# A fused two-block transformer kernel: the start distance of the activation tiles in SBUF, 1024 bytes to 1056 and 2048 to 2080

## What is computed

```python
def first_block(x, ...):
    for l in range(DEPTH):                       # DEPTH = 2
        h = rms_norm(x, norm_mix[l])
        proj = h @ w_in[l]                       # 1024 -> 5120
        ...                                      # two attentions
        mixed = gates[..., :D_MODEL] * y_a + gates[..., D_MODEL:] * y_b
        x = x + mixed @ w_out[l]                 # 1024 -> 1024
        h = rms_norm(x, norm_ffn[l])
        x = x + conv_ffn(h, w_up[l], conv_w[l], conv_b[l], w_down[l])   # 1024 -> 5632, 2816 -> 1024
    return rms_norm(x, norm_final)

def hybrid_layer(x, ...):
    proj = rmsnorm(x, norm_mix_w) @ w_in
    ...                                          # delta rule, recurrence
    x = x + concatenate([gdn_out, lru_out]) @ w_out
    u = jax.nn.relu(rmsnorm(x, norm_mlp_w) @ w_ff1)                     # 1024 -> 4096
    return x + (u * u) @ w_ff2                                          # 4096 -> 1024
```

## Time and profile before

| | us |
|---|---|
| median of three runs | 1054.52 |
| lowest, highest | 1054.43, 1056.76 |
| the profiled execution | 1053.14 |
| its span, first to last instruction | 1051.3 |
| TensorE busy in it | 1038.7 |
| VectorE, ScalarE, GpSimd busy | 719.9, 574.1, 287.2 |

### The profile page before, as it was taken

The page is one execution under the profiler, slowest core; times in us unless marked ns, Lnnn a source line. Parts: engine busy times, 40 slices in busy tenths (PEclk is TensorE's granted clock), DMA queues, the critical chain, the costliest instruction groups (busy, mean ns, idle before and its releaser), DMA issues.

```text
span 1051.3 us, 20017 instructions
## 1 busy us (share of the span) xinstructions
PE 1038.7 (99%) x8398; PEld 984.1 (94%) x8398; DVE 719.9 (68%) x1217; ACT 574.1 (55%) x791; POOL 287.2 (27%) x179
## 2 busy tenths in 40 slices
PE   8999999999999999999999999999999999999997
PEld 7999998999999899999999989998999999899996
DVE  5762248787688775322788967877888789666663
ACT  6454466655355644445765544556658875343443
POOL 0376675100000137666740000013400035001120
PEclk9999999999999999999999999999999999999999
DMA  9644454465763664344455566456432157664841
GB/s 308 202 158 154 157 166 161 161 215 159 228 200 126 208 224 164 124 158 140 156 186 189 173 225 215 133 152 220 122 114 89 61 181 230 191 210 131 261 160 40
DMA packets 169705, 180.11 MB, mean 171 GB/s; under 512 B 4240, under 2 KB 166416, under 8 KB 169488
## 3 DMA queue, kind: packets, MB, share of 16 engines
q1 hardware_dynamic: 169616, 178.84, 52.8%
HBM read 177.78 MB, written 1.05 MB: 170 GB/s over the span
## 4 chain that ended last, share of the span: by engine, by line
PE 84%; DVE 8%; ACT 4%; POOL 2%; issue 1%; DMA 1%; SPq 0%; POOLq 0%; ACTq 0%; DVEq 0%
PE psum L679 83%; DVE sb_w_lo L1861 3%; POOL sb_w_lo L2615 1%; ACT sb_scratch L1329 1%; ACT sb_w_hi L1329 1%; DVE psum L1845 1%; DVE sb_xg_lo L1845 1%; POOL sb_scratch L2655 1%; DVE sb_scratch L1845 1%; DMA sb_raw<-in_w_in 1%; PE psum L906 1%; DVE sb_xt L1879 0%; DVE sb_xt L1877 0%; ACT L1329 0%; DVE sb_hid_both L1936 0%
## 5 line engine op out<-in xcount | busy, mean ns | idle before, releaser
L1329 ACT ACTIVATE sb_w_hi<-sb_raw 128x2048 fp32r<-128x2048 f32 (+3 forms) x185 | 318.7, 1727 | 162.0 <-PE psum L679 98.6
L679 PE MATMUL psum<-sb_xg_hi,sb_w_hi 128*128 128x256 f32 x1656 | 401.8, 283 | 0.4 <-DVE psum L1845 0.3
L679 PE MATMUL psum<-sb_xg_lo,sb_w_hi 128*128 128x256 f32 x1656 | 396.7, 279 | 0.0
L1861 DVE TENSOR_TENSOR sb_w_lo<-sb_raw,sb_w_hi 128x2048 fp32r<-128x2048 f32 (+3 forms) x150 | 305.9, 2042 | 104.4 <-ACT sb_w_hi L1329 103.3
L679 PEld LDWEIGHTS psum<-sb_xg_hi,sb_w_hi 128*128 128x128 f32 x1656 | 310.2, 187 | 3.7 <-issue 0.9
L679 PEld LDWEIGHTS psum<-sb_xg_lo,sb_w_hi 128*128 128x128 f32 x1656 | 310.7, 188 | 0.3
L679 PE MATMUL psum<-sb_xg_hi,sb_w_lo 128*128 128x256 f32 x1656 | 228.4, 280 | 1.0 <-DVE sb_w_lo L1861 0.9
L679 PE MATMUL psum<-sb_hid_both,sb_w_hi 128*128 128x512 f32 (+1 forms) x912 | 210.4, 364 | 0.7 <-DVE sb_hid_both L1936 0.4
L679 PEld LDWEIGHTS psum<-sb_xg_hi,sb_w_lo 128*128 128x128 f32 x1656 | 207.9, 187 | 2.0 <-DVE sb_w_lo L1861 1.4
L2615 POOL TENSOR_TENSOR sb_w_lo<-sb_raw,sb_w_hi 128x2048 fp32r<-128x2048 f32 (+1 forms) x34 | 156.0, 4594 | 107.3 <-ACT sb_w_hi L1329 97.9
L679 PEld LDWEIGHTS psum<-sb_hid_both,sb_w_hi 128*128 128x128 f32 x912 | 148.7, 188 | 22.2 <-DVE sb_hid_both L1936 1.2
(11 more groups left out here) (172 smaller groups left out, 988.4 us busy)
## 6 DMA issues: line engine op xcount, KB each, us to landing
sb_raw<-in_w_in SPq DMA_DIRECT2D x51, 1024.0 KB, 5.2
sb_raw<-in_w_up SPq DMA_DIRECT2D x44, 1024.0 KB, 5.1
sb_raw<-in_w_ff SPq DMA_DIRECT2D x21, 1024.0 KB, 5.6
sb_raw<-in_w_down SPq DMA_DIRECT2D x16, 768.0 KB, 4.9
sb_raw<-in_w_down SPq DMA_DIRECT2D x16, 640.0 KB, 4.4
sb_raw<-in_w_out SPq DMA_DIRECT2D x8, 1024.0 KB, 5.2
sb_raw<-in_w_ff SPq DMA_DIRECT2D x8, 768.0 KB, 4.6
sb_raw<-in_w_ff SPq DMA_DIRECT2D x8, 640.0 KB, 4.5
```

What stands on the lines that cost most here:

```text
L679: return nc.tensor.matmul(ps, lhsT, rhs, start=start, stop=stop, skip_group_check=True)
L1329: return nc.scalar.activation(out_, in_, func, **kw)
L1861: v.tensor_tensor(part(w_lo, s), part(raw, s), part(w_hi, s).bitcast(F32), ALU.subtract)\
```

## The change

`XPITCH = 264` is the distance, in columns, from one tile of `xg_hi` (and of `xg_lo`) to the next: 1056 bytes instead of 1024. Tile i of either is now `xg_of(buf, i)`, the 256 columns from 264·i on; the eight columns between tiles are not used. A pair of `hid_both` begins every 520 columns, 2080 bytes instead of 2048; inside a pair the high and the low part still touch. The writers (ScalarE's copy, VectorE's subtraction) and the readers (`xg_parts`, `hid_pair`) go to the new places. `xg_full`, `xt`, the weights and all else keep their form.

The three buffers grow by 256, 256 and 384 bytes in a partition. `xg_lo` now begins at byte 33152 and `hid_both` at 41600, and everything behind them (`w_hi` and `w_lo` among it) lies 896 bytes higher; `w_lo` ends at 226528. Every engine has the same instructions in the same order with the same waits; only addresses differ.

```diff
--- before.py
+++ after.py
@@ -91,6 +91,7 @@
 RAWS = 1
 IDLE_TURNS = 12
 SLAB = 2048
+XPITCH = 264
 RING = 3
 BANK_SC, BANK_T, BANK_O = 3, 5, 7
 
@@ -405,9 +406,9 @@
             return ctx.enter_context(nc.sbuf_tensor("sb_" + name, [P, cols], dt))[:, :]
 
         xt = sb("xt", KD * T)
-        xg_hi = sb("xg_hi", KD * T, F32R)
-        xg_lo = sb("xg_lo", KD * T, F32R)
-        hid_both = sb("hid_both", 2 * HID * T, F32R)
+        xg_hi = sb("xg_hi", KD * XPITCH, F32R)
+        xg_lo = sb("xg_lo", KD * XPITCH, F32R)
+        hid_both = sb("hid_both", HID * (T + XPITCH), F32R)
         cst = sb("consts", CONSTS.shape[1])
         par = sb("params", PARAM_COLS["cols"])
         sq = sb("sq", 4 * T)
@@ -512,9 +513,13 @@
 
             return plan.banks[plan.at[t][0]][-1] + 1
 
+        def xg_of(buf, i):
+
+            return buf[:, i * XPITCH:i * XPITCH + T]
+
         def hid_pair(i):
 
-            return tl(hid_both, i, 2 * T)
+            return hid_both[:, i * (T + XPITCH):i * (T + XPITCH) + 2 * T]
 
         def hid_hi(i):
             return hid_pair(i)[:, 0:T]
@@ -523,7 +528,7 @@
             return hid_pair(i)[:, T:2 * T]
 
         def xg_parts(i):
-            return tl(xg_hi, i), tl(xg_lo, i)
+            return xg_of(xg_hi, i), xg_of(xg_lo, i)
 
         def hid_parts(first=0):
             return lambda i: (hid_hi(first + i), hid_lo(first + i))
@@ -1369,13 +1374,13 @@
 
                 act.wait_ge(S["x_tile"], q.next("x_tile"))
                 if square_gain:
-                    f(tl(xg_hi, m), tl(xt, m), ACT.Copy, scale=gain(m)).then_inc(S["xg_hi"], 1)
+                    f(xg_of(xg_hi, m), tl(xt, m), ACT.Copy, scale=gain(m)).then_inc(S["xg_hi"], 1)
                 for n in range(2 if square_gain else 1):
                     square_room(m, 2 if square_gain else 1, n)
                     kw = {} if n == 0 else {"scale": square_gain(m)}
                     f(tl(sq, 2 * n + m % 2), tl(xt, m), ACT.Square, **kw).then_inc(S["square"], 1)
                 if not square_gain:
-                    f(tl(xg_hi, m), tl(xt, m), ACT.Copy, scale=gain(m)).then_inc(S["xg_hi"], 1)
+                    f(xg_of(xg_hi, m), tl(xt, m), ACT.Copy, scale=gain(m)).then_inc(S["xg_hi"], 1)
 
             def guess():
 
@@ -1401,7 +1406,7 @@
                 f(tl(xg_full, m), tl(xt, m), ACT.Copy, scale=col("norm_mix0", m)).then_inc(S["xg_full"], q.one("xg_full"))
             for m in range(KD):
                 act.wait_ge(S["xg_full"], m + 1)
-                f(tl(xg_hi, m), tl(xg_full, m), ACT.Copy).then_inc(S["xg_hi"], 1)
+                f(xg_of(xg_hi, m), tl(xg_full, m), ACT.Copy).then_inc(S["xg_hi"], 1)
             for m in range(4):
                 first_square(m)
             split(1)
@@ -1864,7 +1869,7 @@
             def x_low(m, gain):
 
                 dve.wait_ge(S["xg_hi"], q.next("xg_hi"))
-                stt(tl(xg_lo, m), tl(xt, m), gain(m), tl(xg_hi, m).bitcast(F32), ALU.mult, ALU.subtract)\
+                stt(xg_of(xg_lo, m), tl(xt, m), gain(m), xg_of(xg_hi, m).bitcast(F32), ALU.mult, ALU.subtract)\
                     .then_inc(S["xg_lo"], 1)
 
             def x_add(m, t):
@@ -1980,7 +1985,7 @@
                 v.tensor_copy(tl(xt, m), turned(m)).then_inc(S["x_tile"], 1)
             for m in range(KD):
                 dve.wait_ge(S["xg_hi"], q.next("xg_hi"))
-                v.tensor_tensor(tl(xg_lo, m), tl(xg_full, m), tl(xg_hi, m).bitcast(F32), ALU.subtract).then_inc(S["xg_lo"], 1)
+                v.tensor_tensor(xg_of(xg_lo, m), tl(xg_full, m), xg_of(xg_hi, m).bitcast(F32), ALU.subtract).then_inc(S["xg_lo"], 1)
             for m in range(1, 4):
                 add_square(m)
             split(1)
```

## The result

The changed kernel is slower: 1062.93 us at the median of five runs (1061.71 to 1064.91), against 1054.8 for the kernel before, at the median of the five runs beside it. The ratio is 1.0078 with an interval of 1.0063 to 1.0092: 8.1 us. The forecast of no change was wrong; the time is close to what the slower rival named, 1063.7, but the experiments show that its mechanism is not the one at work. It also lies inside the range of 1022 to 1064, by 1 us and only because the range took in that rival: that is luck, not a right account.

What follows compares the result with a forecast made beforehand. TensorE's matmul pace was taken as the bound. All four terms were 0, so 1051.3 + 1.84 + 0 = 1053.1 us, set against the median (1.4 us above the profiled execution) as 1054.5 us; range 1022 to 1064.

Steps and rivals of the forecast that it cites:

- forecast of no change: Whole kernel: the moved tiles do nothing the hardware sees; 1054.5 us, chance 0.50.
- the slower rival: Moving tiles starting 32 bytes past a multiple of 64 cost 3.3 ns each at 3332 starts; 1063.7 us, chance 0.18.
- What bounds the kernel: TensorE, busy 1038.7 of 1051.3 us at full clock: the pace of the matmuls is the time of the kernel.
- The reading of the pace: Up projection: 117.1 ns per 256-column matmul against 106.7, about 10 ns lost, placed along the stream rather than at seams.
- So it isn't the weight load that the stream collides with: Stage with only eight weight columns: ten matmuls at 117.0 ns each, so loading weights was ruled out as the loss.
- Term (1): Seams of the 6008 narrow matmuls: value 0, bounds 10 or 4.7 ns gained and 3.3 ns lost each.
- Term (2): Seams of the 656 wide matmuls: only the start of a pair moves; value 0, same bounds per start.
- Term (3): ScalarE and VectorE writing high and low tiles, 497 and 723 ns: value 0, 1 us if a tenth slower or faster.
- Term (4): Everything behind the activations shifted 896 bytes, hidden under TensorE for DMA and splitting engines: 0, at most 1 us.
- The faster rival: Loss sits at seams in up and input projections; 1013 us, or 1034 if half the seams gain; chance 0.32.
- Its lower price: Gain of 4.7 ns per narrow matmul, from plain fp32 records: 32 in 7.17 us, columns passing four times at 112 ns.
- Its signs in the profile: Odd-numbered tiles follow more slowly than even ones; matmuls with streaming weights stay at 120 and 233 ns.

## Why the prediction was wrong

**What bounds the kernel.** Right. TensorE's pace sets the time; the neighbours and the writers had no part in the loss, the clock none but in the first slab of the one profiled execution, and 1.8 ns on the narrow matmuls came out as 8.1 us.

**The reading of the pace.** 117 ns for 256 columns that need 106.7 was rightly seen as a loss, and rightly as one that goes with the columns. The step that failed is the conclusion: "the loss goes with the columns, not with the starts", hence "a new seam gives nothing". A loss that is spread over the stream can still depend on where the stream lies against the other one. In every row with 128 fp32r weight columns the relation of tile and weights was the same: 32 bytes modulo 256 where the weights stand, 224 where they stream. Rows in which a quantity doesn't vary can't show that it matters; the prediction looked only at places modulo 1024 of one moving tile after another.

**"So it isn't the weight load that the stream collides with"**, from eight weight columns at 117.0 ns, is not borne out. That stage also differs in another thing: with eight columns the chunks lie 32 bytes apart, so the relation steps from chunk to chunk in every kernel. In the kernel with the weights 64 bytes higher the same ten matmuls took 1.13 us:

```profile
726.74 0.28 PE L686 MATMUL psum<-sb_xg_hi,sb_w_hi 128*8 128x256 f32 x1
...
727.87 0.73 PE L686 MATMUL psum<-sb_xg_hi,sb_w_lo 128*8 128x256 f32 x5
```

That is 113 ns each, in a kernel whose pace with 128 weight columns is 118.3. The kernel before, with 117.0 and 116.75, happened to show no difference. So with eight weight columns a stage can be 5 ns faster; whether by the smaller load or by the distance of 32 bytes, no run separates.

**Term (1), the narrow seams, 0.** It measured 1.8 ns for each matmul of `xg_hi` and `xg_lo` and 1.1 ns for those of `hid_both`, inside the bound of 3.3 ns that the prediction had kept for a loss, but not for the reason of that bound. A new seam as such gives and costs nothing (256 bytes, 116.75 ns); a distance that isn't a multiple of 256 costs, on the side of the tiles (118.6 ns) as on that of the weights (118.1). One account is that the change spreads the tiles over all eight relations, whose mean pace is 117.9 ns, where the kernel before had all of them at one of the good ones, 116.75. It leaves 0.6 ns of the 1.8 over, and it isn't shown against the rival that such a step costs by itself.

**Term (2), the wide ones, 0.** Right as measured: 232.6 and 233.0 ns.

**Term (3), the writers, 0.** Right: 723 and 724 ns, 497 and 494.

**Term (4), the shift of the rest by 896 bytes, "0, at most the same 1 us".** This was wrong by itself: the shift of the weights alone costs 4.4 us. The term priced the shift for the DMA and the splitting engines alone and had no cost for TensorE's own reading of the shifted weights. That they stay where they were modulo 128 is no protection: relations 0 and 128 have 119.9 and 118.7 ns, 64 and 192 have 117.5 and 114.7. Terms (1) and (4) don't add: in the changed kernel another 96 bytes brought nothing (118.6 ns).

**The faster rival** fell in its place (the seam), yet the loss is partly one of position, as it supposed: one relation in eight gives 113.3 ns in most output tiles. Its lower price rested on a misreading of the earlier trace rows: 7.17 us is the length of the records up to the end of the last. The next matmul starts 6.82 us after the first, and most starts in between lie 216 ns apart, so by the prediction's own count of four passes the columns of plain fp32 go by at 108 ns and not at 112, and the bound was 8.7 ns where it has 4.7.

**The slower rival** came within 1 us of the time by another mechanism. Its starts at half of 64 bytes are refuted twice: without any such start the kernel is as slow (1.0059), and with nothing but such starts it is nearly as before (1.0016). The 3.3 ns that it took from the earlier trace rows belong to another relation and to a standing tile read in another pattern. Its signs in the profile had been named as odd tiles slower than even ones and streaming weights unchanged. The first holds in half: in the passes of the high weights the odd tiles were slower, 120.3 ns against 117.7 (before the change 117.4 against 115.9), in those of the low weights they were faster, 117.4 against 118.3. And where the last product streams `w_hi`, the matmuls got faster, from 233.2 to 231.1 ns on the mean. The standing tiles there are spread by the change too; that this is the reason isn't shown.

**The rule of the skill.** The Trainium skill, SBUF — State Buffer, section "Who interferes with whom", has TensorE waiting on no one. That holds against the other engines here, by the earlier trace rows. But the place of the moving tile against the standing weights changes TensorE's pace by up to 5.2 ns in 256 columns (114.7 to 119.9); whether that is one of its reads waiting for the other, no run shows.

## What to carry to other kernels

Where fp32r tiles stream through TensorE and the starts come more slowly than the columns need, the place of the moving tile against the standing one is a free parameter: in this kernel one empty buffer of 96 bytes was worth 0.8%. In the runs here distances that are a multiple of 256 bytes, on both sides, were needed to keep the pace of one relation; so keep to them, and then try the eight offsets. And when a change lengthens a buffer, everything behind it moves: test that shift alone before the cost is put down to the change.

## What the runs showed of the hardware

- The pace of a matmul of 256 fp32r columns at the granted clock 1.00 (2.4 GHz) lay between 113.3 and 120.0 ns over output tiles with undisturbed starts and equal relations, by the place of the moving tile against the standing weights modulo 256 bytes; a step of 256 bytes between tiles changed nothing (116.75 ns, ratio 1.0003). Why these places and paces, no run here shows.
- 16 bytes make a difference: 118.7 ns at relation 176, between 117.8 at 160 and 114.7 at 192.
- At relation 192 two paces stand side by side in one execution, 113.3 ns in 95 output tiles and 117.8 or 117.9 in 39, and a stretch keeps its own.
- With eight weight columns, 32 bytes apart, ten matmuls of 256 columns took 1.13 us where those with 128 weight columns ran at 118.3 ns (relation 224).
- Places that step by 32 bytes on both sides, with the relation kept at 32, don't keep its pace: 118.5 ns instead of 116.75.
- The best place for matmuls of 512 columns is another (229.0 ns at relation 64, 231.5 to 233.5 elsewhere) than for those of 256.
